# A hybrid decoder layer on Trainium2: 112 filler slabs of one projection counted over eight iterations, 15 in each of seven and 7 in the eighth, in place of 16 in each of seven

## What is computed

```python
mod = silu(c) @ w_ada + b_ada             # 2048 x 12288: shift, scale, gate (twice)
h = rmsnorm(x) * (1 + scale1) + shift1
z = h @ w_in                              # Z_A columns for mixer A, the rest for B and gates
z_a, q_b, k_b, v_b, gate_a, gate_b = split(z)
y_a = rwkv7(z_a)                          # 16 heads, state 64 x 64
o_b = moba(q_b, k_b, v_b, cached pages)   # block-sparse attention
x = x + gate1 * ((sigmoid(gate_a) * (y_a @ w_proj_a) + sigmoid(gate_b) * (o_b @ w_proj_b)) @ w_out)
x = x + gate2 * conv_ffn(rmsnorm(x) * (1 + scale2) + shift2)
```

## Time and profile before

| | |
|---|---|
| median of 3 runs | 2553.3 us (2551.41 to 2555.43) |
| the profiled execution's own time | 2563.09 us |
| its span in the profile | 2561.2 us |
| mean granted TensorE clock | 0.954 |
| busy: PE, PEld, DVE, ACT, POOL | 93%, 81%, 44%, 38%, 4% |
| first tanh of iterations 0 and 7 | 332.8 and 1047.4 us |

### The profile page before, as it was taken

One profiled execution on the slowest core, in us unless ns is written; L12 is line 12 of the kernel. 1 busy time (PEld: TensorE's weight loads), 2 busy tenths in 40 slices (PEclk: granted clock), 3 DMA queues, 4 the chain that ended last, 5 costly groups with the idle time before them and its releaser, 6 DMA issues.

```text
span 2561.2 us, 50616 instructions
## 1 busy us (share of the span) xinstructions
PE 2378.6 (93%) x19850; PEld 2077.1 (81%) x19850; DVE 1125.2 (44%) x1805; ACT 965.8 (38%) x1402; POOL 105.3 (4%) x224
## 2 busy tenths in 40 slices
PE   6899999999999999867898899979999999999997
PEld 2289978878878878535566699979999999999996
DVE  1333354354443543434323454465555555544435
ACT  1133343333342443325444233345454555433332
POOL 0000010000000000100000000001010101000000
PEclk8999989999999999958888799989999999999998
DMA  9865455665656666642788544435555555554442
GB/s 272 298 191 164 138 165 170 195 189 176 190 178 190 181 186 187 227 145 79 256 313 301 178 150 160 136 122 166 164 164 164 165 166 166 166 166 165 165 151 91
DMA packets 327417, 460.77 MB, mean 180 GB/s; under 512 B 37633, under 2 KB 208915, under 8 KB 326803
## 3 DMA queue, kind: packets, MB, share of 16 engines
q1 hardware_dynamic: 319645, 450.39, 55.5%
q10 hardware_dynamic: 7634, 8.38, 0.9%
HBM read 442.83 MB, written 15.86 MB: 179 GB/s over the span
## 4 chain that ended last, share of the span: by engine, by line
PE 80%; DVE 8%; DMA 5%; ACT 2%; SPq 2%; issue 1%; DVEq 0%; ACTq 0%; POOL 0%
PE ps L1893 75%; DMA raw<-in_w_ada 4%; PE ps L2405 3%; DVE v_px L1649 1%; DVE wlo L1521 1%; DVE srow L1753 0%; DVE smg L1745 0%; DVE rkv L1492 0%; DVE wlo L1369 0%; SPq L694 0%; ACT kT L915 0%; DVE srow L1743 0%; DVE sq L1379 0%; PE ps L2424 0%; DVE smg L1754 0%
## 5 line engine op out<-in xcount | busy, mean ns | idle before, releaser
L915 ACT ACTIVATE whi<-raw 128x1024 fp32r<-128x1024 f32 x496 | 524.8, 1059 | 890.1 <-PE ps L1893 861.8
L1893 PE MATMUL ps<-hhi,whi 128*128 128x288 f32 x2752 | 835.5, 304 | 15.4 <-DVE hlo L1413 12.6
L1893 PE MATMUL ps<-hhi,wlo 128*128 128x288 f32 x2752 | 813.8, 296 | 0.0
L1893 PE MATMUL ps<-hlo,whi 128*128 128x288 f32 x2752 | 813.3, 296 | 0.0
L1369 DVE TENSOR_TENSOR wlo<-raw,whi 128x1024 fp32r<-128x1024 f32 x384 | 470.1, 1225 | 659.9 <-ACT whi L915 659.8
L1893 PEld LDWEIGHTS ps<-hhi,whi 128*128 128x128 f32 x2752 | 519.1, 189 | 60.2 <-issue 39.8
L1893 PEld LDWEIGHTS ps<-hlo,whi 128*128 128x128 f32 x2752 | 519.4, 189 | 1.2
L1893 PEld LDWEIGHTS ps<-hhi,wlo 128*128 128x128 f32 x2752 | 519.0, 189 | 0.0
L1893 PE MATMUL ps<-fhi,wlo 128*128 128x288 f32 x704 | 207.7, 295 | 0.0
L1893 PE MATMUL ps<-fhi,whi 128*128 128x288 f32 x704 | 207.7, 295 | 0.0
L1893 PE MATMUL ps<-flo,whi 128*128 128x288 f32 x704 | 207.3, 294 | 0.0
(11 more groups left out here) (374 smaller groups left out, 2738.5 us busy)
## 6 DMA issues: line engine op xcount, KB each, us to landing
raw<-in_w_ada SPq DMA_DIRECT2D x192, 512.0 KB, 4.8
raw<-in_w_up SPq DMA_DIRECT2D x352, 256.0 KB, 2.9
raw<-in_w_in SPq DMA_DIRECT2D x160, 512.0 KB, 4.1
raw<-in_w_down SPq DMA_DIRECT2D x88, 512.0 KB, 3.6
kpage<-in_cache_k SPq DMA_DIRECT2D x64, 512.0 KB, 5.2
kpage<-in_cache_v SPq DMA_DIRECT2D x64, 512.0 KB, 4.9
raw<-in_w_out SPq DMA_DIRECT2D x32, 512.0 KB, 3.6
raw<-in_w_proj_a SPq DMA_DIRECT2D x16, 512.0 KB, 3.7
```

The lines of the kernel that those rows point to most:

```text
L915: return act.activation(o, i, ACT.Copy, **k)
L1893: return pe.matmul(out, lhsT, rhs, start=start, stop=stop, **k)
```

## The change

The 112 slabs are numbered through, i = 15 j + k, and a helper `rest_step(i)` places the evacuations and the spills by that number: evacuation of group (i - 2) // 4 ahead of a slab with i % 4 == 1, spill behind one with i % 4 == 2. Iterations 0 to 6 use places k = 0 to 14, iteration 7 uses k = 0 to 6, and ScalarE goes on counting there to k = 9 for the last evacuation and spill. SyncE's loops are written out; in iteration 7 the modulation slabs keep to two buffers.

```diff
-RG, RS = 4, 16
+RS, RL = 15, 7
+assert RS * (KA - 1) + RL == REST // 2 * 4
...
             def both_slabs(j, s0, s1):
                 for s in range(s0, s1):
-                    rest_slab(j, s)
+                    if s < (RS if j < KA - 1 else RL):
+                        rest_slab(j * RS + s)
                     ada_slab(j, s)
...
-            with sp.Fori(0, 1) as j:
...
-            with sp.Fori(1, KA - 1) as j:
+            for j in range(KA - 1):
                 both_slabs(j, 0, 3)
                 lora_loads(j)
                 both_slabs(j, 3, 6)
-                pair_stores(j - 1)
+                if j:
+                    pair_stores(j - 1)
                 both_slabs(j, 6, 13)
                 state_loads(j)
-                both_slabs(j, 13, RS)
+                both_slabs(j, 13, ADA_J)
...
             for s in range(ADA_J):
-                idx = ADA_1 * ADA_K + j * ADA_J + s
-                src = wsrc(d["w_ada"], s % ADA_K * 2 * P, j * (2 * CH) + (ADA_1 + s // ADA_K) * CH, CH)
-                if s < 4:
-                    wait = ((ada_used, idx - 1), (slab_lo, n1 - 1), (ada_used, idx - 2), (slab_lo, n1))[s]
-                else:
-                    wait = (ada_used, idx - 3)
-                slab(s, 0, 0, src, wait)
+                both_slabs(j, s, s + 1)
                 if s == 5:
                     pair_stores(j - 1)
                 if s == 9:
-                    sp.wait_ge(spilled, 16 * RG * (KA - 1))
+                    sp.wait_ge(spilled, 16 * (REST // 2))
                     sp.wait_ge(slab_used, n1)
...
+            def rest_step(i, read=True):
+
+                if read and i % 4 == 1 and i > 4:
+                    rest_evac((i - 2) // 4)
+                if i < REST // 2 * 4:
+                    rest_hi(i)
+                if i % 4 == 2 and i > 4:
+                    rest_spill((i - 2) // 4 - 1)
...
                 def fill(i):
-                    if dense:
-                        rest_hi(j, i)
+                    if i < (RS if j < KA - 1 else RL + 3):
+                        rest_step(j * RS + i)
...
-                fill(15)
+                if j < KA - 1 and (j * RS + RS) % 4 == 1:
+                    rest_evac((j * RS + RS - 2) // 4)
                 ada_rows2(j, 1)
...
-                if more:
-                    rest_hi(j, RS)
+                if j < KA - 1:
+                    rest_step(j * RS + RS, False)
                 act.wait_ge(ya_done, j + 1)
                 act.activation(yahi[:, jc, :].rearrange("p o t -> p (o t)"), v_thw[:, :], ACT.Copy).then_inc(ya_hi, 1)
-                if dense:
-                    rest_evac(j, 3)
-                    rest_spill(j, 3)
...
                 def fill(i, half):
-                    if dense:
-                        rest(j, i, half)
+                    if i < (RS if j < KA - 1 else RL):
+                        rest(j * RS + i, half)
```

More of the change, by code:

```diff
@@ L506, in build @@
         n = 0
-        for name, ks, groups in (("za", 8, 7), ("rest", RS, KA - 1), ("merge", 8, 4), ("out", 8, 4),
+        for name, ks, groups in (("za", 8, 7), ("rest", REST // 2 * 4, 1), ("merge", 8, 4), ("out", 8, 4),
                                  ("up", 8, 22), ("down", 22, 4)):
@@ L638, in ada_slab, with rest_slab @@
                 sp.dma_start(raw[:, r, :, :], src).then_inc(slab_in[r], 16)
-            def rest_slab(j, i):
+            def rest_slab(i):
                 r, n = 1 + 2 * (i % 2), stages["rest"][0] + i
-                src = d["w_in"][i % 4 * CH:i % 4 * CH + CH, bass.ds(j * (RG * RW) + (ZA + i // 4 * RW), RW)].rearrange("(t p) n -> p t n", p=P)
-                sp.wait_ge(slab_lo, j * RS + (n - 1))
+                col = ZA + i // 4 * RW
+                src = d["w_in"][i % 4 * CH:i % 4 * CH + CH, col:col + RW].rearrange("(t p) n -> p t n", p=P)
+                sp.wait_ge(slab_lo, n - 1)
                 sp.dma_start(quads(raw[:, r, :, :]), src).then_inc(slab_in[r], 16)
@@ L781, in landed @@
             v, per = 16 * (before // 4 + n // 4 + 1), 4
+            if name not in ("za", "rest"):
+                v += (16 if n % 2 == 0 else -16) * (ADA_J // 4)
             if name == "up":
@@ L1013, in _, with rest_hi, rest_evac, rest_spill @@
                 copy(nshn[:, 4 * b * P:4 * b * P + w], pbank(b)[0:NC, 0:w]).then_inc(last_rows, 1)
-            def rest_hi(j, i):
+            def rest_hi(i):
                 r, n = 1 + 2 * (i % 2), stages["rest"][0] + i
-                act.wait_ge(slab_in[r], j * (RS * 8) + 16 * (REST_IN + i // 2 + 1))
-                act.wait_ge(slab_used, j * RS + (n - 1))
+                act.wait_ge(slab_in[r], 16 * (REST_IN + i // 2 + 1))
+                act.wait_ge(slab_used, n - 1)
                 copy(whi[:, n % 2, :, :], raw[:, r, :, :]).then_inc(slab_hi, 1)
-            def rest_evac(j, q):
-                act.wait_ge(slab_used, j * RS + (stages["rest"][0] + 4 * q + 4))
-                act.wait_ge(spilled, j * (16 * RG) + 16 * q)
+            def rest_evac(g):
+                act.wait_ge(slab_used, stages["rest"][0] + 4 * g + 4)
+                if g:
+                    act.wait_ge(spilled, 16 * g)
                 copy(restev[:, :, :], ps[:, 5:7, 0:T]).then_inc(rest_out, 1)
-            def rest_spill(j, q):
-                act.wait_ge(rest_out, j * RG + (q + 1))
-                act.dma_start(spill[one(j, 2, 2 * RG, 2 * q), :, :].rearrange("t p f -> p t f"), restev[:, :, :]).then_inc(spilled, 16)
+            def rest_spill(g):
+                act.wait_ge(rest_out, g + 1)
+                act.dma_start(spill[2 * g:2 * g + 2, :, :].rearrange("t p f -> p t f"), restev[:, :, :]).then_inc(spilled, 16)
+            def rest_step(i, read=True):
[5 more added lines that the diff above has]
+                    rest_spill((i - 2) // 4 - 1)
             def ada_rows2(j, half):
@@ L1033, in ada_rows2, with rwkv @@
                 copy(adr[:, :], pbank(7)).then_inc(ada_copied, 1)
-            def rwkv(j, dense, more):
+            def rwkv(j):
                 jc = one(j)
@@ L1089, in rwkv @@
                             copy(Tf[h, :, :, h].rearrange("p e c t -> p (e c) t"), TT[h, :, :, :].rearrange("p e c t -> p (e c) t"))
[L1090 to L1095, removed]
                     fill(lev + 5)
@@ L1125, in rwkv @@
                 right_sides(1)
-                if dense:
-                    rest_evac(j, 2)
                 fill(13)
                 solved(1)
-                if dense:
-                    rest_spill(j, 2)
                 fill(14)
@@ L1146, in rwkv @@
                 act.activation(v_px[:, :], pbank(0)[:, 0:T], ACT.Sqrt, bias=c("eps_lnx"), scale=1.0 / HEAD_A).then_inc(gn_roots, 1)
-                if more:
-                    rest_hi(j, RS)
+                if j < KA - 1:
+                    rest_step(j * RS + RS, False)
                 act.wait_ge(ya_done, j + 1)
                 act.activation(yahi[:, jc, :].rearrange("p o t -> p (o t)"), v_thw[:, :], ACT.Copy).then_inc(ya_hi, 1)
-                if dense:
-                    rest_evac(j, 3)
-                    rest_spill(j, 3)
-            rest_hi(0, 0)
+            rest_hi(0)
             act.wait_ge(last_rows, 7)
@@ L1159, in _ @@
             for j in range(KA):
-                rwkv(j, j < KA - 1, j < KA - 2)
+                rwkv(j)
             def plain(name, u=None, added=None, ends={}):
@@ L1516, in mix_pair, with rest_lo, rwkv @@
                 i.then_inc(mixed, 1)
-            def rest_lo(j, i):
+            def rest_lo(i):
                 r, n = 1 + 2 * (i % 2), stages["rest"][0] + i
-                dve.wait_ge(slab_hi, j * RS + (n + 1))
+                dve.wait_ge(slab_hi, n + 1)
                 TTn(wlo[:, n % 2, :, :], raw[:, r, :, :], whi[:, n % 2, :, :].bitcast(F32), ALU.subtract).then_inc(slab_lo, 1)
-            def rwkv(j, dense, more):
+            def rwkv(j):
                 def fill(i):
-                    if dense:
-                        rest_lo(j, i)
+                    if i < (RS if j < KA - 1 else RL):
+                        rest_lo(j * RS + i)
                 r_, k_, v_ = rkv[:, 0, :], rkv[:, 1, :], rkv[:, 2, :]
@@ L1658, in rwkv @@
                 ada_cols(2 * j + (ADA_1 + 1), 2 * j + (ADA_1 + 2), 7)
-                if more:
-                    rest_lo(j, RS)
+                if j < KA - 1:
+                    rest_lo(j * RS + RS)
             own(dve.memset(Tf[64:P, :, :, 0:64], 0.0))
             mix_pair(0, 0)
-            rest_lo(0, 0)
+            rest_lo(0)
             for j in range(KA):
-                rwkv(j, j < KA - 1, j < KA - 2)
+                rwkv(j)
             def fl(ap):
@@ L2043, in ada @@
                         pe.wait_ge(ada_in_mod, 2 * j + (ADA_1 + s // ADA_K))
[L2044 to L2049, removed]
+                    r = 2 * (s % 2)
+                    pe.wait_ge(slab_in[r], 16 * (REST_IN + (j * ADA_J + s) // 2 + 1))
                     for kt in range(2):
@@ L2054, in ada, with rest @@
                     i.then_inc(ada_used, 1)
```

(16 more changed lines are left out.)

6 lines of the change are left out of this document (removed).

## The result

The changed kernel takes 2598.1 us (median of 4 runs, 2593.04 to 2604.98) against 2552.7 us of the kernel before on the same chip: a ratio of 1.0178, 95% interval 1.0153 to 1.0204, or 45 us more. Forecast were 2586 us, 33 more. The profiled execution took 2597.2 us, where that of the kernel before took 2563.1, 10 above its median; the two traces therefore differ by 34 us only.

The account below looks back on a forecast made before the run. TensorE, holding 80% of the chain of waits, was taken to bound the kernel. Terms -6 + 9.3 - 4 + 6 + 19.5 + 8 = +32.8 on 2553.3 us gave 2586 us, range 2563 to 2602.

Parts of the forecast that it names:

- The removed slab 15: Six handovers: PE loses a slab of 3.35 us but waits 3.2 us for v_sq; -6 us, bounds -4 and -10.
- Evacuations: Iterations 1 to 6: PE waits for ScalarE's copies at the new places; +9.3 us, bounds 4 and 12.
- SyncE's loops: Written-out loops shorten PEld's waits for modulation slabs; -4 us, bounds -6 and 0.
- The clock at the handovers: Clock falls over one fill(0) at four of six handovers, about 1.5 us each; +6 us, bounds 0 and 11.
- Seven slabs, and the reload: Eighth iteration: seven slabs cost +19.5 us; late gate reload makes PE stand 10.3 us instead of 2.5, +8.
- The rival with 15 for this term: Clock falls at every handover, twice in some iterations: clock term 15, reload 12, +46, 2600 us; chance 0.14.

Follow-up runs that it names:

- two runs with the squares first: VectorE forms v_kk, v_sq and the next remainder ahead of the reciprocal: kernel before with SyncE's loops written out, 2562.6 us; changed kernel, 2610.7 us.
- run with work in the gap: Changed kernel plus 20 matmuls nobody reads behind the lora products of iterations 1 to 7: 2584.3 us, ratio 1.0101 to the kernel before.
- both repairs: Changed kernel with 20 unread matmuls behind the lora products of iterations 1 to 7 and gates reloaded behind modulation slab 15: 2574.9 us, ratio 1.0072.
- run with 12 and 4 slabs: Changed kernel with 16 slabs in six iterations, 12 in the seventh, 4 in the eighth, evacuations at their old places: 2571.6 us, ratio 1.0056.

## Why the prediction was right, and where it was off

The sign, and 33 of 45 us, came out of the right mechanisms. Step by step:

- *The removed slab 15.* Right. PE waits 3.07 us for v_sq where 3.2 was forecast, at every handover; -23.5 and +16.4 make -7.1, forecast -6. The two runs with the squares first added that this way of having v_sq earlier does not help.
- *Evacuations.* +9.3 forecast, 9.8 us of waits in 14 places. The run without them left it open how much of that the whole kernel feels. The longest is the one I named, at the start of iteration 4: 1.6 us where 2.5 was forecast, and 2.2 in the run with work in the gap, where the clock is up.
- *SyncE's loops.* -4 forecast; measured alone, -3.9 in the waits of PE up to the eighth iteration and -3.8 in the whole runs.
- **The clock at the handovers** is the step that was mis-sized: +6, "four of six" at "about 1.5". It fell at six of six, and cost 2.5 us a time, up to 3.2, for it covers the v_sq product and the matmuls of fill(0). The 1.5 did not follow from the rows either: a pair of modulation slabs takes 0.87 us more per 1.07, and by that ratio a slab of 3.35 us costs 2.7. The whole term is 15 us, above even my bound of 11. The run with work in the gap gave back 15.7 in its trace and 20 by the whole runs. The Trainium skill (TensorE: Matmul & The Clock Gate, section HAM oscillation), by which a wait that is long enough costs the upper rate at every burst, agreed with the trace: all seven handovers paid, at 3.07 us. The rival with 15 for this term had its size, though not by its reason: no second fall in an iteration was needed.
- *Seven slabs, and the reload.* 27.5 forecast, 25.4 in the trace. Both places, 48 us behind the product and a wait near 10 us, were right. From the v_sq product PE comes to slab 10 after 55.6 us (54.8 forecast), 20.4 later than before; 2.5 of these are the seventh handover's fall of the clock, which my sum left out: in the run with work in the gap, without that fall, it is 17.9 where 19.5 was forecast. The wait for slab 10 grew by 8.5 us, forecast 8. From slab 10 to the end of yalo it took 3.4 us less than before, where I had let it run as before; the clock is up again sooner there, and the last pair of modulation slabs takes 1.13 us in place of 1.94.

With 15 for the clock the sum up to the eighth product is 14.3, where the traces show 13.4, and the whole sum 42, against 45 by the medians. That the traces differ by 34 us and the forecast was 33 is luck: 8 too little up to the eighth product, 2 too much in the eighth iteration, and 5 shorter behind it. That 42 agrees with 45 is partly luck too: the stages behind the eighth iteration were 4.7 us shorter in the changed kernel's profile, with unchanged code, and the kernel before was profiled in an execution 10 us above its median. I can't place those 10 us. In the traces of all versions the part ahead of the first tanh takes 329 to 341 us and that behind the eighth yalo 1435 to 1443, with the same instructions, so totals of single traces can't be read finer than that.

What stays open is the eighth iteration. After both repairs 18 us remain over the kernel before. The run with 12 and 4 slabs shows that slabs there lose by themselves, and that the lower clock lasts longer with them; how much of the 19 us is the slabs and how much the clock wasn't separated. What makes the clock fall there is not shown either: the long wait is not needed for it, and dense unread work put it off.

## To carry to other kernels

When filler work is moved from a full place to one that looks empty, price what its absence leaves behind: a wait in the place it came from, and the clock of the work behind that wait, counted over all the instructions that run at the lower level and not by one sample of them. Idle time in a thin, chained stretch is not free room for transfers and dense work; read which transfer is gated by the last piece moved. A cheap test for the clock is to fill the gap with work that nobody reads: if the kernel gets faster, the clock was a loss. Pick the type of that work on purpose, and count what it takes in the trace.

## What the runs showed of the hardware

- A stand of TensorE of 3.07 us between dense stretches was followed, seven times out of seven, by the lower clock over about one slab; behind stands of 0.85 us it stayed at 1.00 over 611 us. With 20 unread matmuls, 2.9 us, in the gap it stayed up too.
- The lower clock in the eighth iteration needs no single long wait: with the 2.48 us wait taken away it fell some 8 us sooner in the iteration, and the stretch from 1080 to 1100 us had the same 0.56. The longest wait of TensorE ahead of that fall was 1.4 us.
- A matmul of 288 columns with plain float32 operands took 0.56 us (72 of them, 144 records, 40.5 us) where one of the fill slabs' rounded type follows the next in 0.13 us, both at a granted clock of 1.00.
- SyncE's issues from written-out code instead of a register loop took 3.9 us of waiting for transfers off TensorE over seven iterations.
